# The order of a projection and mLSTM head loop, of an output projection and of a closing norm, rewritten; low halves and token shifts on GpSimd

## The chip, the cores and the metric

The program runs on one core of a Trainium2 chip. The metric is the device time of one execution in microseconds. An execution is one step of a small decoder layer over 576 tokens, 512 of a prompt and 8 sequences of 8 sample tokens.

## The reference, cut to what matters

```python
def mlstm_chunkwise(q, k, v, ig, lf, C0, n0, m0):      # per head and chunk of tokens
        m_t = jnp.maximum(log_inter, jnp.max(log_d, axis=-1))
        d = jnp.exp(log_d - m_t[..., None])
        s_inter = jnp.exp(log_inter - m_t)
        qk = jnp.einsum('bhtd,bhsd->bhts', qc, kc) * d
        num = s_inter[..., None] * jnp.einsum('bhtd,bhde->bhte', qc, C) + jnp.einsum('bhts,bhse->bhte', qk, vc)
        ...
        C_new = s_state[..., None, None] * C + jnp.einsum('bhs,bhsd,bhse->bhde', w_chunk, kc, vc)

def rwkv7_mixer(cols, shift0, S0, mu, ...):
    prev = jnp.concatenate([shift0[:, None, :], cols[:, :-1]], axis=1)
    xs = cols + (prev - cols) * mu                     # the token shift
    ...
    kk = kk / jnp.maximum(jnp.linalg.norm(kk, axis=-1, keepdims=True), 1e-12)

def hybrid_layer(x, ...):
    cols = (rmsnorm(x, norm_mix_g) @ w_in).astype(f32)
    ...
    x = x + mix @ w_out
    x = x + peer(rmsnorm(x, norm_ffn_g), peer_w_q, peer_sub_keys, peer_u, peer_v)
```

and at the end `y = rmsnorm(x, norm_final_g)`. Four mLSTM heads of width 128 and eight RWKV heads, worked in four pairs, share the input projection `w_in`. `peer` is a product-key mixture of single-row experts.

## The kernel before, in words

Activations stand transposed, channels on partitions and tokens along the free dimension. float32 products are taken as three products of a rounded high half and a low half: ScalarE writes the high half of a weight panel, another engine writes the low half as raw minus high.

**Stage A, the projection jobs and the heads.** The input projection is a list `JOBS`. The first 23 (`NF`) give q, k, v and o. The last 14 are of kind "r", one for each 128 RWKV columns; each is 48 matmuls of 128x288 on a narrow panel. There are two panel slots `narrow[0]` and `narrow[1]`: the load of panel j waits until job j-2 is done, `narrow_high` makes its high half on ScalarE and `narrow_low` its low half on VectorE (L1815). Every "r" job writes banks 0 and 1 and begins only when ScalarE has copied the bank of the job ahead of it (`copy_job`, L806 to L808). GpSimd then scales the copied columns by the rows' norm (L678, L679).

The list `BESIDE` says how many "r" jobs follow each part of the four heads. On TensorE a head is `decays` (six matmuls, L1226 to L1232), `keys` (transposes of the keys and the key-query products), `updates` (L1256, L1258), `numerators` (L1266 to L1271) and `head_back` (transposes, L1278). Between them VectorE does the state update (`cn`, `cnS`), the convolution of the next head (`conv`, L1893, L1895), the head norm's statistics and the product with `sg` (`silu`); ScalarE does the decay weights (exponentials, L876, L877), sigmoids (L815, L904), the norm's root (L913) and the normalised rows `hs_t` (L920). `decays(h + 1)` waits for `hs_ready` of head h, since it writes banks 2 and 3 that `hs_t` reads. In head 3 VectorE also makes the channel tensors of the first RWKV pair (`prep_first`: shifts, `decay_sums`, `kk_clamp`, a reciprocal at L1990, products up to L2011), ahead of the last two jobs' columns and behind them. The pair loop then begins with transposes (L1432, L1436) and the gram products (L1444). GpSimd makes the channel tensors of pairs 1 to 3 (`prep`).

**Stage B, the output projection.** Ten products of 8 matmuls each, first the left halves of the five token tiles (`FTILES`), then the right halves (L1635). VectorE adds each to the rows (L2311), then norms all tiles (L2316, L2319), TensorE transposes them (L1663), and the 16 query jobs follow (L1689, L1690).

**Stage C, the end.** The last expert sums run over eight column banks c = 0 to 7. VectorE copies each bank out (L2604), TensorE transposes all back (L1783), and per token tile VectorE adds two halves (L2614), ScalarE squares and takes a root (L1161, L1162), VectorE takes a reciprocal and scales (L2618, L2619), and a DMA writes the tile out. Engines run their own queues in the order in which the code is written; semaphores join them.

## Time and profile before

| | us |
|---|---|
| median of 3 runs (lowest, highest) | 2225.6 (2223.4, 2240.89) |
| the profiled execution, its own time | 2228.57 |
| its span, from the first to the last instruction | 2226.7 |
| mean granted clock of TensorE in it | 0.956 of full speed |

Times in the rows below are microseconds from the start of that span. A row of the timeline is: start, busy time, engine, line, operation, output and inputs, and in square brackets the idle time of the engine ahead of it with what ended it. "x48" is the number of instructions run together. The clock 1.0 stands for 2.4 GHz, 0.5 for 1.2 GHz; a number between them is a mean over a stretch.

### The profile page before, as it was taken

What the parts mean: (1) busy time and instruction counts of PE and PEld (TensorE: products, weight loads), DVE (VectorE), ACT (ScalarE), POOL (GpSimd) and SP (SyncE); (2) the same over time, 40 slices, a digit from 0 to 9 for tenths busy, and PEclk for the clock granted to TensorE, in tenths of its full rate; (3) what the DMA queues carried; (4) which work ended last, traced back from release to release, by engine and by line L of the source; (5) the groups of instructions that cost most, each with busy time, mean ns of one, the idle gap of its engine ahead of it and who ended that gap; (6) DMA issues with size and microseconds to landing.
All of it is one profiled execution on the core that took longest, in us unless ns stands there. A gap on an engine that the chain in (4) does not pass through costs nothing.

```text
span 2226.7 us, 35721 instructions
## 1 busy us (share of the span) xinstructions
PE 2072.9 (93%) x14513; PEld 1818.7 (82%) x14513; DVE 1549.0 (70%) x2689; ACT 752.3 (34%) x924; POOL 549.1 (25%) x473
## 2 busy tenths in 40 slices
PE   7999778778899998999999999999999999999995
PEld 7988657656646778888889889989899999999995
DVE  6435656556424888888898889897776666677664
ACT  5334334333112003334444544544322222222221
POOL 8111106541000000032242242122423233332320
PEclk9999868788999999999999999999999999999998
DMA  5121210002121213577797788679988888888872
GB/s 184 58 61 49 59 36 3 7 2 83 50 109 43 76 38 128 187 245 262 270 366 277 255 326 304 236 276 357 373 317 310 311 323 308 306 304 305 312 253 88
DMA packets 175771, 437.45 MB, mean 196 GB/s; under 512 B 12192, under 2 KB 92832, under 8 KB 165280
## 3 DMA queue, kind: packets, MB, share of 16 engines
q1 hardware_dynamic: 127552, 242.81, 31.5%
q0 software_dynamic: 36864, 134.23, 16.2%
q10 hardware_dynamic: 11232, 58.73, 6.5%
q8 instruction: 82, 1.34, 0.2%
q14 instruction: 41, 0.34, 0.0%
HBM read 368.57 MB, written 67.17 MB: 196 GB/s over the span
## 4 chain that ended last, share of the span: by engine, by line
PE 59%; DVE 11%; issue 1%; ACT 1%; DMA 0%; POOL 0%; ACTq 0%; DVEq 0%
PE bank L1770 28%; PE bank L1708 23%; PE bank L1717 3%; PE bank L1635 3%; DVE sc L2330 1%; DVE si L2329 1%; DVE si L2332 1%; DVE isel L2472 1%; DVE sv L2328 1%; DVE sv L2331 1%; DVE u_lo L2337 1%; DVE sca L2343 1%; DMA sca<-in_pu_rows,pick 0%; ACT u_hi L1068 0%; PE bank L1689 0%
## 5 line engine op out<-in xcount | busy, mean ns | idle before, releaser
L1708 PE MATMUL bank<-xhi,u_hi 128*128 128x448 f32 x1024 | 386.3, 377 | 8.8 <-DVE u_lo L2337 8.2
L1770 PE MATMUL bank<-w_hi,v_hi 128*128 128x448 f32 x1024 | 375.1, 366 | 5.5 <-DVE w_lo L2575 5.5
L1708 PE MATMUL bank<-xhi,u_lo 128*128 128x448 f32 x1024 | 375.9, 367 | 0.0
L1708 PE MATMUL bank<-xlo,u_hi 128*128 128x448 f32 x1024 | 375.2, 366 | 0.0
L1770 PE MATMUL bank<-w_lo,v_hi 128*128 128x448 f32 x1024 | 374.8, 366 | 0.0
L1770 PE MATMUL bank<-w_hi,v_lo 128*128 128x448 f32 x1024 | 374.8, 366 | 0.0
L725 POOL DMA_INDIRECT sca<-in_pu_rows,pick x128 | 169.8, 1326 | 733.2 <-DVE sdot L2343 447.2
L725 POOL DMA_INDIRECT rows_v<-in_pv,pick x128 | 196.4, 1535 | 430.6 <-DVE xs L2557 383.2
L2581 DVE TENSOR_TENSOR v_lo<-v_raw,v_hi 128x4096 fp32r<-128x4096 f32 x32 | 141.6, 4425 | 172.4 <-ACT v_hi L1129 172.4
L1129 ACT ACTIVATE v_hi<-v_raw 128x4096 fp32r<-128x4096 f32 x32 | 116.1, 3627 | 429.0 <-PE bank L1770 426.3
L1708 PEld LDWEIGHTS bank<-xhi,u_hi 128*128 128x128 f32 x1024 | 193.1, 189 | 24.1 <-issue 7.9
L1770 PEld LDWEIGHTS bank<-w_hi,v_hi 128*128 128x128 f32 x1024 | 193.0, 189 | 21.2 <-issue 5.9
L1708 PEld LDWEIGHTS bank<-xhi,u_lo 128*128 128x128 f32 x1024 | 193.8, 189 | 17.8
L1708 PEld LDWEIGHTS bank<-xlo,u_hi 128*128 128x128 f32 x1024 | 193.7, 189 | 15.3
L1770 PEld LDWEIGHTS bank<-w_lo,v_hi 128*128 128x128 f32 x1024 | 193.1, 189 | 15.3
L1770 PEld LDWEIGHTS bank<-w_hi,v_lo 128*128 128x128 f32 x1024 | 192.9, 188 | 15.3
L2337 DVE TENSOR_TENSOR u_lo<-u_raw,u_hi 128x2048 fp32r<-128x2048 f32 x64 | 146.5, 2290 | 61.9 <-ACT u_hi L1068 61.6
L1076 ACT ACTIVATE actb<-bank 128x448 f32<-128x448 f32 x128 | 69.8, 545 | 348.7 <-PE bank L1708 341.6
L2557 DVE SCALAR_TENSOR_TENSOR xs<-rows_v,sdot,xs 128x1024 f32<-128x1024 f32 x127 | 162.7, 1281 | 10.8 <-DMA rows_v<-in_pv,pick 3.7
L2343 DVE CUSTOM_DVE_ANT_0 sca<-sca,xs 128x1024 f32<-128x1024 f32 x128 | 151.7, 1220 | 19.0 <-DMA sca<-in_pu_rows,pick 18.6
L1068 ACT ACTIVATE u_hi<-u_raw 128x2048 fp32r<-128x2048 f32 x64 | 123.2, 1926 | 23.2 <-issue 9.1
L1097 ACT ACTIVATE gst<-bank 128x512 f32<-128x512 f32 x112 | 125.2, 1146 | 15.5 <-PE bank L1717 11.7
(619 smaller groups left out, 3486.4 us busy)
## 6 DMA issues: line engine op xcount, KB each, us to landing
u_raw<-in_pu SPq DMA_DIRECT2D x64, 1024.0 KB
v_raw<-in_pv SPq DMA_DIRECT2D x32, 2048.0 KB, 16.7
act_scratch<-actb ACTq DMA_DIRECT2D x64, 448.0 KB
gate_scratch<-gst ACTq DMA_DIRECT2D x14, 2048.0 KB, 9.1
wts<-act_scratch SPq DMA_DIRECT2D x32, 896.0 KB, 4.7
gring<-gate_scratch SPq DMA_DIRECT2D x32, 896.0 KB, 8.6
wring<-in_w_q SPq DMA_DIRECT2D x4, 2048.0 KB, 8.5
wp_raw<-in_w_in SPq DMA_DIRECT2D x7, 1024.0 KB, 5.5
```

What stands on the lines that cost most here:

```text
L725: pool.indirect_dma_start(dst, None, rows[:, :], bass.IndirectOffsetOnAxis(pick[:, s:s + 1], 0)).then_inc(s_row[s % RING], 16)
L1068: act.activation(u_hi[:, g % 2, :, :], u_raw[:, g % 2, :, :], ACT.Copy).then_inc(S("u_hi_ready"), 1)
L1076: act.activation(actb[:, q, e, :], bank[b][:, 0:DS], ACT.Gelu).then_inc(S("dot_banks_free"), 1)
L1097: act.activation(gst[:, c % 2, :, o:o + 4].rearrange("p a t -> p t a"), bank[5 + k % 2][:, :].rearrange("p (t a) -> p t a", t=4), ACT.Copy ...
L1129: act.activation(v_hi[g % 2][:, :], v_raw[g % 2][:, :], ACT.Copy).then_inc(S("v_hi_ready"), 1)
L1635: return mm(bank[jj % 6][0:n, :], mixT[:, kt, t0:t0 + n], w_o[:, half, kt, :], start=kt == 0, stop=kt == KD - 1)
L1708: ins = mm(bank[b][:, 0:DS], lhsT, rhs[:, 0:DS], **on)
L1770: ins = mm(bank[c][:, 0:DS], lhsT, rhs[q][:, e, :], **on)
L2337: TT(u_lo[:, g % 2, :, :], u_raw[:, g % 2, :, :], u_hi[:, g % 2, :, :].bitcast(f32), ALU.subtract).then_inc(S(f"u_lo_ready{g % 2}"), 1)
L2343: dve.tensor_tensor_reduce(rows_u[s % RING], rows_u[s % RING], xs[:, :], 1.0, 0.0, ALU.mult, ALU.add, sdot[:, s:s + 1]).then_inc(S("row_us ...
L2557: STT(out=accS[:, :], in0=rows_v[:, s % RING, :], scalar=sdot[:, s:s + 1], in1=accS[:, :], op0=ALU.mult, op1=ALU.add).then_inc(S("row_adde ...
L2581: TT(v_lo[q][:, :], v_raw[q][:, :], v_hi[q][:, :].bitcast(f32), ALU.subtract).then_inc(S("v_lo_ready"), 1)
```

## The change

**Stage A.** On TensorE, `decays(h + 1)` moves up behind `numerators(h)` and waits for `p_ready` and `cn_ready`; the numerators get banks 6 and 7. Head 3 has no jobs of its own: its two jobs run in head 2, with the first pair's small products `lora_decay` and `lora_rate` between them. In `keys` the products come first. The first pair's `bonus_sums` comes behind the transposes of the pair loop. On GpSimd come all 14 low halves, each ahead of the scaling of the job before, and the shifts of the first pair and of the two gate inputs; `prep_first` is gone, and what is left of it is written into head 3 on VectorE. On ScalarE the decay weights of head h + 1 and a high half come ahead of the root and `hs_t` of head h, and the copy of one job's bank comes behind `hs_t`.

**Stage B.** The output projection goes tile by tile, the adds, norms and transposes of a tile follow while the next is multiplied, and the first two query jobs are split into two token halves around the last two tiles' transposes.

**Stage C.** Token tile 4 is finished first, banks are turned back as they are copied, the left and right halves are squared apart, and ScalarE scales the left half.

```diff
@@ -665,40 +668,73 @@
 
             pool.wait_ge(s_low, LOW["rms"])
             rb_seq = rb[:, SEQ:NT].rearrange("p (b s) -> p b s", b=NB)
-            for ji, (kind, _, _, d) in enumerate(JOBS):
+            def narrow_low(j):
+
+                if j == 0:
+                    pool.wait_ge(s_low, LOW["w7"])
+                if j < 14:
+                    pool.wait_ge(s_high, HIGH[f"n{j}"])
+                    raw, hi, lo = narrow[j % 2]
+                    pool.tensor_tensor(lo[:, :, :], raw[:, :, :], hi[:, :, :].bitcast(f32), ALU.subtract).then_inc(s_low, 1)
+
+            TT, TSC = pool.tensor_tensor, pool.tensor_scalar
...
+            def shifted(dst, ct):
+                seq, own_seq = [a.rearrange("p (b s) -> p b s", b=NB) for a in (ext_r[:, ct, 1 + SEQ:], dst[:, SEQ:NT])]
+                cur, prev = ext_r[:, ct, 1:1 + SEQ], ext_r[:, ct, 0:SEQ]
+                TT(dst[:, 0:SEQ], prev, cur, ALU.subtract)
+                link(TT(own_seq, seq[:, :, 0:NS], seq[:, :, 1:], ALU.subtract))
+                link(TSC(dst[:, :], dst[:, :], pcol("mu", ct), None, ALU.mult))
...
+
+            for ji, (kind, i, _, d) in enumerate(JOBS):
                 if kind in "gv":
                     continue
+                if ji == FIRST[7]:
+                    narrow_low(0)
+                if kind == "r":
+                    narrow_low(i + 1)
                 pool.wait_ge(s_pe, ji + 1)
...
+                if kind == "r" and i in (1, 9, 10, 13):
+                    pool.wait_ge(S("scaled"), 12 + i + 1)
+                if kind == "r" and i == 1:
+                    pool.wait_ge(S("rows_ready"), 1)
+                    shifted(xwa, 12)
+                    shifted(xg, 13).then_inc(S("lora_in"), 1)
+                if kind == "r" and i == 9:
+                    pool.wait_ge(S("conv_ready"), 8)
+                    link(shifted(X["r"], 0))
+                if kind == "r" and i == 10:
+                    link(shifted(X["k"], 4))
+                    link(TSC(X["kk"][:, :], X["k"][:, :], pcol("k_k", 0), None, ALU.mult))
+                if kind == "r" and i == 11:
+                    TT(X["t"][:, :], X["kk"][:, :], X["kk"][:, :], ALU.mult).then_inc(S("kk_squares"), 1)
+            shifted(XP[0]["v"], 8)
+            pool.wait_ge(S("decay_ready"), 1)
+            TT(ARP[0][:, 1, :], X["r"][:, :], X["cum"][:, :], ALU.mult).then_inc(S("scaled"), 1)
+
...
             jobs = iter(range(NF, NJ))
-            for h in range(MLH):
+
+            def decay_weights(h):
                 act.wait_ge(S("decays_done"), h + 1)
...
+            decay_weights(0)
+            highs = iter(range(1, 14))
+            narrow_high(next(highs))
+            copy_job(next(jobs))
+            for h in range(MLH):
                 if h:
...
                     act.activation(mixT[:, 0:4, :], mixT[:, 0:4, :], ACT.Sigmoid)
-                if h == 2:
...
+                if h + 1 < MLH:
+                    decay_weights(h + 1)
+                    narrow_high(next(highs))
                 act.wait_ge(S("stats_step"), 2 * h + 1)
                 act.activation(sm[:, 3, :], sm[:, 2, :], ACT.Sqrt, bias=eps_t[:, 0:1]).then_inc(S("std_ready"), 1)
                 own(S("std_ready"))
...
@@ -917,18 +951,26 @@
                     act.wait_ge(S("head_back"), h)
                 for t, (t0, n) in enumerate(TILES):
                     o = 129 * (t % 3)
-                    last = act.activation(hs_t[0:n, t, :], bank[2 + t // 3][0:n, o:o + 128], ACT.Identity,
+                    last = act.activation(hs_t[0:n, t, :], bank[6 + t // 3][0:n, o:o + 128], ACT.Identity,
                                           scale=sm[0:n, 4, t:t + 1], bias=sm[0:n, 5, t:t + 1])
                 last.then_inc(S("hs_ready"), 1)
                 own(S("hs_ready"))
-                if BESIDE[h][3]:
-                    copy_r(next(jobs))
+                if h < 3:
+                    copy_job(next(jobs))
+                    narrow_high(next(highs))
+                if h == 2:
+                    lora(1, "sw", "w0", 0)
+                if h < 3:
+                    copy_job(next(jobs))
+                if h == 2:
+                    lora(2, "av", "a0", 0)
+                    copy_job(next(jobs))
...
+                act.wait_ge(S("y_ready"), t + 2)
+                act.activation(x1_late[t][0:n, halves[0]], y_half[t][0:n, :], ACT.Copy, scale=st[0:n, t, 3:4]
                                ).then_inc(S("yrms_ready"), 1)
                 own(S("yrms_ready"))
+            for t, (t0, n) in enumerate(FTILES[0:4]):
+                act.wait_ge(S("x2_ready"), t + 6)
+                link(act.activation(sq_late[0:n, halves[1]], x1_late[t][0:n, halves[1]], ACT.Square, accum_out=st[0:n, t, 0:1]))
+                act.activation(st[0:n, t, 3:4], st[0:n, t, 0:1], ACT.Sqrt, bias=st[0:n, t, 2:3], scale=1.0 / D
+                               ).then_inc(S("yrms_ready"), 1)
+                own(S("yrms_ready"))
+                if t:
+                    half_out(t - 1)
+            half_out(3)
 
...
             def keys(h):
                 pe.wait_ge(S("qk_ready"), h + 1)
+                pe.wait_ge(S("qs_ready"), h + 1)
+                for t, (t0, n) in enumerate(TILES):
+                    dst = bank[2][:, 128 * t:128 * t + 128] if t < PT else bank[3][0:n, 0:n]
+                    ins = mm(dst, kh[:, t0:t0 + n], qh[:, t0:t0 + n], start=True, stop=True)
+                ins.then_inc(S("qk_done"), 1)
...
+                    dst = bank[6 + t // 3][0:n, 129 * (t % 3):129 * (t % 3) + 129]
...
             jobs = iter(range(NF, NJ))
             decays(0)
+            job(next(jobs))
             for h in range(3):
-                for part, n_jobs in zip((None, keys, updates, numerators), BESIDE[h]):
-                    if part:
-                        part(h)
-                    for _ in range(n_jobs):
-                        job(next(jobs))
+                keys(h)
+                job(next(jobs))
+                updates(h)
+                job(next(jobs))
+                numerators(h)
                 decays(h + 1)
+                job(next(jobs))
+                if h == 2:
+                    lora_decay(0)
+                job(next(jobs))
+                if h == 2:
+                    lora_rate(0)
+                    job(next(jobs))
                 head_back(h)
-
-            early = prep(0)
-            next(early)
             keys(3)
-            next(early)
-            next(early)
+            kk_sums(0)
+            pe.wait_ge(S("kk_stage"), 1)
             updates(3)
-            pe.wait_ge(S("lora_out"), 2)
-            job(next(jobs))
-            next(early)
             numerators(3)
-            pe.wait_ge(S("kk_stage"), 1)
...
+                if p == 0:
+                    pe.wait_ge(S("mix_ready"), 4)
+                    bonus_sums(0)
...
+                t, half = divmod(jj, 2)
...
             pe.wait_ge(S("mix_ready"), 8)
+            def turn_back(t):
+
+                n = FTILES[t][1]
+                pe.wait_ge(S("xf_ready"), t + 1)
+                if t == 1:
+                    pe.wait_ge(S("x1_ready"), 6)
+                if t >= 2:
+                    pe.wait_ge(S("xfT_ready"), t - 1)
+                for kt in range(KD):
+                    ins = pe.transpose(bank[6 - 2 * (t % 2) + kt // 4][:, n * (kt % 4):n * (kt % 4) + n],
+                                       xf_rows(t)[0:n, 128 * kt:128 * kt + 128], ident[0:n, 0:n])
+                ins.then_inc(S("xfT_done"), 1)
+
...
                 for kt in range(KD - 1 if jj < 6 else 0, KD):
                     ins = out_product(jj, kt)
                 ins.then_inc(S("outproj_done"), 1)
-            for t, (t0, n) in enumerate(FTILES):
-                pe.wait_ge(S("xf_ready"), t + 1)
-                if t >= 2:
...
+            def q_half(j, half):
...
+            for j in range(2):
+                q_half(j, 0)
+                turn_back(3 + j)
             pe.wait_ge(S("xfT_ready"), 5)
-            pe.wait_ge(S("x1_ready"), 10)
...
+                q_half(j, 1).then_inc(S("qproj_done"), 1)
             def scores(j):
...
@@ -1769,6 +1883,15 @@
                                       skip_group_check=True)
                             ins = mm(bank[c][:, 0:DS], lhsT, rhs[q][:, e, :], **on)
                     ins.then_inc(S("sum_done"), 1)
+                    if last and c == 4:
+                        pe.wait_ge(S("sum_banks_free"), 4)
+                        for t in range(4):
+                            turn_half(t, range(0, 4), 0).then_inc(S("back_done"), 1)
+                    if last and c == 6:
+                        pe.wait_ge(S("sum_banks_free"), 6)
+                        pe.wait_ge(S("x2_ready"), 5)
+                        for t in range(4):
+                            turn_half(t, range(4, 6), 1)
...
+                turn_half(t, (6,), 1)
             pe.wait_ge(S("sum_banks_free"), KD)
-            for t, (t0, n) in enumerate(FTILES[0:4]):
...
+                turn_half(t, (7,), 1).then_inc(S("back_done"), 1)
 
 
...
+            add_rows(0)
+            add_rows(1)
+            add_rows(2)
+            dve.wait_ge(s_sub, 32)
+            norm_rows(0)
+            norm_rows(1)
+            add_rows(3)
+            norm_rows(2)
+            norm_rows(3)
+            add_rows(4)
+            norm_rows(4)
...
+            for c in range(1, 5):
+                bank_out(c)
+            for t in range(4):
+                add_half(t, 0)
+            for t in range(4):
+                n = FTILES[t][1]
+                TT(y_half[t][0:n, :], x1_late[t][0:n, 0:512], gain[0:n, 0:512], ALU.mult)
+                if t in (0, 2):
+                    bank_out(5 + t // 2)
+            bank_out(7)
+            add_half(0, 1)
+            for t in range(1, 4):
+                add_half(t, 1)
+                scale_rows(t - 1, slice(512, D), ROOT[t])
+            scale_rows(3, slice(512, D), ROOT[4])
 
 
```

TensorE's queue from the last products of numerators(0) on, before (L1178 is a job, L1226 to L1232 are decays(1), L1278 is head_back(0)):

```order
L1178 MATMUL bank<-xhi_b,wn_lo 128x288 x2
L1226 MATMUL bank<-row_E,selr 128x512 [waits cn_ready,hs_ready]
L1227 MATMUL bank<-row_E,selr 128x64
L1228 MATMUL bank<-row_E,selr 128x512
L1229 MATMUL bank<-negm,ident 128x512
L1231 MATMUL bank<-row_E,selr 64x64
L1232 MATMUL bank<-negs,ident 64x64
L1278 MATMUL bank<-ident,hs_t 128x128 [waits hs_ready]
```

The same place after; the job (L1255) now follows decays(1), which no longer waits for `hs_ready`:

```order
L1343 MATMUL bank<-vaug,dpm 64x129
L1348 MATMUL bank<-cn,qsX 64x129 x8
L1303 MATMUL bank<-row_E,selr 128x512 [waits cn_ready,p_ready]
L1304 MATMUL bank<-row_E,selr 128x64
L1305 MATMUL bank<-row_E,selr 128x512
L1306 MATMUL bank<-negm,ident 128x512
L1308 MATMUL bank<-row_E,selr 64x64
L1309 MATMUL bank<-negs,ident 64x64
L1255 MATMUL bank<-xlo,wn_hi 128x288 [waits proj_copied,low_halves_ready]
```

The decays moved ahead of one job, and head_back(0) stands behind that and another one.

ScalarE's queue behind the convolution of head 1, before (`mixT` is the output gate's sigmoid, `sm` the norm's root, `dpm` the decay weights, `wn_hi` a high half, `ext_r` a job's copy):

```order
L904 ACTIVATE mixT<-mixT 128x2304 [waits scaled,conv_sig]
L913 ACT_TABLE_LOAD
L913 ACTIVATE sm<-sm,eps_t 128x5 [waits stats_step]
L920 ACTIVATE hs_t<-bank,sm 128x128 [waits stats_step,std_ready]
L920 ACTIVATE hs_t<-bank,sm 128x128 x3
L920 ACTIVATE hs_t<-bank,sm 64x128
L763 ACTIVATE wn_hi<-wn_raw 128x1024 [waits w_narrow_loaded0,hs_ready]
L806 ACTIVATE ext_r<-bank 128x288 [waits proj_done]
L807 ACTIVATE ext_r<-bank 128x224
L808 ACTIVATE ext_r<-bank 128x8x8
```

and after:

```order
L935 ACTIVATE mixT<-mixT 128x2304 [waits scaled,conv_sig]
L908 ACT_TABLE_LOAD [waits p_ready]
L908 ACTIVATE dpm<-bank,mcol 128x128 [waits decays_done]
L908 ACTIVATE dpm<-bank,mcol 128x128 x3
L909 ACTIVATE dpm<-bank,mcol 64x64
L799 ACTIVATE wn_hi<-wn_raw 128x1024 [waits w_narrow_loaded0,d_ready]
L947 ACT_TABLE_LOAD
L947 ACTIVATE sm<-sm,eps_t 128x5 [waits stats_step]
L954 ACTIVATE hs_t<-bank,sm 128x128 [waits stats_step,std_ready]
L954 ACTIVATE hs_t<-bank,sm 128x128 x3
L954 ACTIVATE hs_t<-bank,sm 64x128
L842 ACTIVATE ext_r<-bank 128x288 [waits proj_done,hs_ready]
```

The exponentials and a high half stand ahead of the root, and a job's copy stands behind `hs_t` and waits for `hs_ready`.

GpSimd's queue around the second "r" job; before, only L678 and L679 stood here:

```order
L678 TENSOR_TENSOR wn_lo<-wn_raw,wn_hi 128x1024 [waits high_halves_ready]
L705 TENSOR_TENSOR ext_r<-ext_r,rb 128x512 [waits proj_copied]
L706 TENSOR_TENSOR ext_r<-ext_r,rb 128x8x8
L685 TENSOR_TENSOR xwa<-ext_r 128x512 [waits rows_ready,scaled]
L686 TENSOR_TENSOR xwa<-ext_r 128x64
L687 TENSOR_SCALAR xwa<-xwa,par 128x576 [waits gpsimd_step]
L688 TENSOR_TENSOR xwa<-xwa,ext_r 128x512 [waits gpsimd_step]
L689 TENSOR_TENSOR xwa<-xwa,ext_r 128x64
```

A low half, the job's scaling, and then two shifts of five operations each, the first of which is shown.

## Rows read from the trace of the kernel before

**Rows 1.** The page, busy time of each engine over the whole span

```profile
PE 2072.9 (93%) x14513; PEld 1818.7 (82%) x14513; DVE 1549.0 (70%) x2689; ACT 752.3 (34%) x924; POOL 549.1 (25%) x473
```

**Rows 2.** Windows: length, busy PE, PEld, DVE, ACT, POOL, clock, DMA share, GB/s

```profile
137.00:146.00 9.00, 8.89 (x55) 8.89 (x56) 3.73 (x9) 2.65 (x8) 0.00 (x0) 0.77 0.04 12
156.54:204.78 48.24, 43.82 (x282) 38.23 (x281) 25.42 (x64) 19.95 (x39) 6.41 (x8) 0.89 0.20 58
204.78:252.93 48.15, 43.83 (x281) 38.02 (x280) 29.83 (x71) 17.82 (x38) 6.39 (x8) 0.89 0.20 56
252.93:340.51 87.58, 64.95 (x363) 53.44 (x364) 54.80 (x135) 30.08 (x59) 9.41 (x11) 0.75 0.14 43
322.00:338.00 16.00, 3.60 (x15) 2.26 (x14) 12.82 (x21) 0.78 (x3) 2.04 (x2) 0.61 0.25 86
678.00:690.00 12.00, 7.77 (x46) 6.52 (x47) 7.72 (x12) 7.81 (x14) 0.00 (x0) 0.86 0.55 199
2198.00:2227.00 29.00, 3.95 (x34) 3.45 (x32) 14.28 (x21) 8.50 (x16) 0.00 (x0) 0.64 0.22 81
```

**Rows 3.** Timeline of PE in the projection and head loop

```profile
137.11 0.85 PE L1178 MATMUL bank<-xlo,wn_hi 128*128 128x288 f32 x2 [1.68 <-DVE wn_lo L1815]
...
153.58 1.05 PE L1256 MATMUL bank<-wv,ktok 128*128 128x129 f32 x8
...
156.54 0.53 PE L1178 MATMUL bank<-xlo,wn_hi 128*128 128x288 f32 x2
...
163.02 0.61 PE L1266 MATMUL bank<-vaug,dpm 128*128 128x129 f32 x4
...
177.98 1.47 PE L1226 MATMUL bank<-row_E,selr 4*128 4x512 f32 x2 [4.42 <-ACT hs_t L920]
...
279.45 2.07 PE L1226 MATMUL bank<-row_E,selr 4*128 4x512 f32 x2 [7.46 <-ACT hs_t L920]
```

**Rows 4.** Timeline of ACT behind head 0 and in front of head 1

```profile
171.58 2.13 ACT L904 ACTIVATE mixT<-mixT 128x2304 f32<-128x2304 f32 x1
...
176.09 1.83 ACT L920 ACTIVATE hs_t<-bank,sm 128x128 f32<-128x128 f32 x5 [0.78 <-DVE sm L2120]
...
184.47 1.28 ACT L876 ACT_TABLE_LOAD   x1 [4.79 <-issue]
185.76 1.14 ACT L876 ACTIVATE dpm<-bank,mcol 128x128 f32<-128x128 f32 x4
```

**Rows 5.** Timeline of DVE, head 0 and then head 3

```profile
160.33 1.23 DVE L1815 TENSOR_TENSOR wn_lo<-wn_raw,wn_hi 128x1024 fp32r<-128x1024 f32 x1
...
164.41 1.14 DVE L1893 TENSOR_SCALAR pre<-ext_q,par 128x64 f32<-128x64 f32 x1
...
169.50 0.31 DVE L1893 TENSOR_SCALAR pre<-ext_q,par 128x64 f32<-128x64 f32 x1
...
170.80 0.16 DVE L2102 COPY den<-bank 128x3 f32<-128x3 f32 x1
...
319.71 3.75 DVE L1990 RECIPROCAL rw_t<-rw_t 128x576 f32<-128x576 f32 x1
...
334.45 0.82 DVE L2011 SCALAR_TENSOR_TENSOR rw_t<-rw_r,par,rw_k 128x576 f32<-128x576 f32 x1
```

**Rows 6.** Timeline of POOL, two-input operations at three places

```profile
69.63 2.80 POOL L678 TENSOR_TENSOR ext_q<-ext_q,rb 128x512 f32<-128x512 f32 x1 [3.26 <-ACT ext_q L808]
...
164.07 1.43 POOL L678 TENSOR_TENSOR ext_r<-ext_r,rb 128x512 f32<-128x512 f32 x1 [8.08 <-ACT ext_r L808]
...
338.73 1.04 POOL L687 TENSOR_TENSOR cn<-ext_r 128x512 f32<-128x512 f32 x1 [13.45 <-DVE mixT L1942]
```

**Rows 7.** Timeline of DVE and PE at the end of the program

```profile
2198.28 0.62 DVE L2604 COPY mixT<-bank 128x448 f32<-128x448 f32 x1 [1.81 <-PE bank L1770]
...
2198.96 3.71 PE L1783 MATMUL bank<-ident,mixT 128*128 128x128 f32 x32 [0.72 <-DVE mixT L2604]
...
2222.42 1.28 DVE L2619 SCALAR_TENSOR_TENSOR v_raw<-v_raw,st,gain 128x1024 f32<-128x1024 f32 x1
```

More of the change, by code:

```diff
@@ L1312, in prep @@
                     pe.wait_ge(S("gate_out"), p - 1)
-                main_and_rest(blk[:, :], X["t"], "bonus_done")
+                channel_product(p, blk[:, :], X["t"], "bonus_done", rest_of(1))
+            def prep(p):
+                lora_decay(p)
+                yield
+                yield
+                lora_rate(p)
+                yield
+                kk_sums(p)
+                for _ in range(14):
+                    yield
+                bonus_sums(p)
                 yield
@@ L2186, in post @@
                 yield
-            for _ in early:
-                pass
+            bonus(0)
             c_md = 0
@@ new lines, in scale_rows, with add_half @@
+            def scale_rows(t, cs, root):
+                n = FTILES[t][1]
+                dve.wait_ge(S("yrms_ready"), root)
+                link(dve.reciprocal(st[0:n, t, 3:4], st[0:n, t, 3:4]))
+                STT(out=x1_late[t][0:n, cs], in0=x1_late[t][0:n, cs], scalar=st[0:n, t, 3:4], in1=gain[0:n, cs], op0=ALU.mult,
+                    op1=ALU.mult).then_inc(S("y_ready"), 1)
+                own(S("y_ready"))
+            def add_half(t, half):
+                n, cs = FTILES[t][1], slice(512 * half, 512 * half + 512)
+                dve.wait_ge(S("back_done"), 4 * half + t + 1)
+                TT(x1_late[t][0:n, cs], bank[t][0:n, :], x1_late[t][0:n, cs], ALU.add).then_inc(S("x2_ready"), 1)
+                own(S("x2_ready"))
```

352 lines of the change are left out of this document (143 added, 209 removed).

## The prediction

> **What bounds the kernel now.** I read the page first: TensorE is busy for 93% of the span [rows 1]. The rest is the budget of any reordering: idle time, and time at the lower clock. So I went to the windows and looked only at the stages that the diff touches [rows 2]. The projection and head loop costs 48.24, 48.15 and 87.58 us for three parts, cut where the `updates` of heads 0, 1 and 2 end and at the first gram product. TensorE is idle for 4.4, 4.3 and 22.6 us of them, and the clock is 0.89, 0.89 and 0.75. Last I read on the timeline what ended each idle time [rows 3]. It is the same in each head: `decays(h+1)` waits for `hs_t`, 4.42 us at 177.98 and 7.46 at 279.45. At 137.11 the first job waits 1.68 for its low half. From 322 to 338 TensorE works 3.60 of 16 us, under VectorE's products for the first pair. Stage B holds 4.2 idle us between 678 and 690, stage C has 3.95 of work in 29 [rows 2].
>
> **The durations I use.** A job is 6.48 us at the full clock (156.54 to 163.02), `updates` 2.96 (153.58 to 156.54), and one pass of 128 columns 0.131 (1.05 for 8) [rows 3]; so `keys` with 15 passes is about 2.0 and `head_back` with 5 about 0.65, both estimates. A restart after a gap also costs clock: the nine microseconds from 137 have a mean of 0.77, so 4.1 us ran at 1.2 GHz and about 2.0 us of work were lost [rows 2]. I take 1.75 for a job that follows an idle time.
>
> **Stage A, the start: −3.5.** The low half of the first panel is now made on GpSimd before TensorE needs it, so the wait of 1.68 goes, and with it most of the 2.0 of slow clock. Nothing else is due there.
>
> **Stage A, head 0: +2.1.** `decays` no longer waits for `hs_t`. But the fourth job of a head needs a bank that ScalarE copies behind `hs_t`, and so the wait returns one job and one `decays` later. What counts is the chain from the end of `updates` to that copy. VectorE: from 156.54 to 170.80 it makes the state and the convolution, 14.26 us; the low half of 1.23 leaves it and so does 0.83 of the row at 164.41 (1.14, where the same operation takes 0.31 at 169.50), so 12.2 [rows 3, 5]. ScalarE: the sigmoid of 0.78 up to 171.58, `mixT` 2.13, the decay weights that now come ahead (table load 1.28, exponentials 1.14, with the small one 2.6), a high half of 1.1 (estimate from `mixT`, 1024 of 2304 columns), table load, root and wait 2.38 up to 176.09, `hs_t` 1.83, the copy 0.8 (estimate, as the sigmoid of 576 columns): 11.6 [rows 4]. To this comes what GpSimd takes from VectorE. The rows at 164 show an exclusion: GpSimd's scaling took 1.43 there, the same kind 1.04 alone at 338.73 and 2.80 at 69.63, and VectorE's row at 164.41 lost 0.83 [rows 5, 6]. In head 0 GpSimd now has, beside the convolution, the four two-input operations of the second shift (estimate 2.7, twice 1.04 and twice a small one), a low half (2.2, an estimate from 1.04 for 512 columns) and a scaling (1.4): 6.3. I take all of it as lost. The chain is 12.2 + 6.3 + 11.6 = 30.1, against some 21 of TensorE's own work, so it stands for nine. Behind it come a job, `head_back`, `keys`, a job and `updates`, 18.6 by the durations above, and 1.75 of clock: 50.4 against 48.24 [rows 2]. Bounds: 44.1 with no exclusion (−4.2), and 53.9 if the slow clock lasts as it does now: 0.11 of 48.24 is 5.3 [rows 2], 3.5 more than 1.75 (+5.6).
>
> The Trainium skill, page "SBUF — State Buffer", section "Who interferes with whom", says that VectorE and GpSimd share one pair of ports and that it is "an exclusive lock": two-input VectorE instructions meet GpSimd's reads there, and those in a two-port mode block it for the whole instruction. The rows agree, in both directions (1.14 for 0.31, 2.80 for 1.04) [rows 5, 6]. The rule speaks against the change, which sends two-input work to GpSimd beside VectorE's own. By the rule head 0 comes to +2.1, as in my sum; without it, to −4.2.
>
> **Stage A, head 1: −2.0.** The same chain with 3.0 of exclusion (a low half, 0.8 of a scaling) and 10.8 on ScalarE, where the two gate inputs take the place of `mixT`: 12.2 + 3.0 + 10.8 + 18.6 + 1.75 = 46.3, against 48.15 [rows 2]. Bounds −5 and +1.7.
>
> **Stage A, heads 2 and 3 to the first gram product: −13.8.** Now four jobs (25.9) run behind head 2's `updates`, and with `numerators`, `decays`, the small products, `head_back`, `keys` and about 1 of waiting (together 16.6, estimates by passes) TensorE reaches `updates(3)` after 42.5. From there the way is serial: `updates` 3.0, the state 3.7, the reciprocal of 3.75 and three products of 0.8 [rows 5], 6.7 with the waits; statistics, root, three more products and `hs_t`, 8.1; then `head_back`, the transposes, `bonus_sums` and 2.5 for a slow clock, 9.8. That is 73.8 against 87.58 [rows 2]. The gain comes from two places: the two jobs that stood in head 3 at half clock now run at full clock without a gap, and the shifts of the first pair and `AR[:,1]` no longer stand in VectorE's row up to 334.45 [rows 5]. Bounds: 68 (VectorE's products hidden under `updates`) and 80 (the low clock lasts).
>
> Of GpSimd's later duty: `prep(1)` starts 2.8 later against the first gram, since the first pair's `bonus` now gates it together with the transposes. I put +1.0 there, between 0 and 2. **Stage A in all: −3.5 + 2.1 − 2.0 − 13.8 + 1.0 = −16.2**, with −23 and −8 as ends that do not all fall together.
>
> **Stage B: −2.7.** Of 12.00 us TensorE works 7.77 [rows 2]. The waits for all adds, then for all norms, go; the two query halves run beside the last tiles' transposes. What cannot go is the last tile's add, root, norm, transposes and copy; beside them there are two half query jobs of about 2.6 us together. I leave 1.5 idle. Bounds −1 (the halves wait as long for the third tile's columns) and −4.5.
>
> **Stage C: −13.2.** Before, the last copy ends at 2198.90 and five rounds of add, square, root and scale are serial through two engines, until 2223.70; the span ends 3.0 later, with the DMA [rows 7]. After, 24 of 32 transposes stand ahead of the last bank's sums, 2.8 of 3.71 [rows 7]: this is a cost, since TensorE is the bound there. The copy ends at 2201.7, the last four transposes 0.8 later, the first half add (0.65, half of 1.28) at 2203.2. Then ScalarE is the bound: it is busy for 8.50 in this window for five tiles with a table load [rows 2], so 1.44 a tile; the half that it no longer squares is replaced by the half that it scales, and I add 0.35 for waits, 1.8. Four tiles end at 2210.5, the DMA at 2213.5, against 2226.7. Bounds: 1.5 a tile (−14.4), 2.3 a tile (−11.2).
>
> **The sum** is −16.2 − 2.7 − 13.2 = −32.1, so 2196.5 for an execution like the profiled one of 2228.57. The median lies 3.0 below that one, so **2193.5**.
>
> **Rivals.** *The wait in the heads only moves.* The new wait behind `hs_t` is as long as the old one, the clock falls and comes back as slowly as now, so that each of three heads costs 3.5 more: −21.6, 2204. For it: nine idle us in head 0 are twice 4.42, and the restart at 177.98 was slow [rows 2, 3]. Against it: what follows the gap is now a dense job instead of small products. 0.2. *GpSimd and VectorE do not exclude each other in these places*, by chance of timing: 6.3 + 3.0 less, 2184. For it: the row of 1.43 is only 0.4 longer than 1.04 [rows 6]. 0.13. *GpSimd's low halves become the bound (slower).* A job waits for its low half. The price: a low half of 2.2 has some 2 us of slack where two jobs follow each other; if each were stretched as the row of 2.80 is against 1.04 [rows 6], by 2.7, it would take 5.9, and 14 of them would cost 14 × 1.7 = 24 us. The change turns to a loss from 6.5 us each on; at 7.5 it costs 46, and the time is 2240. Against it: VectorE is busy for 25.42 of 48.24 us only [rows 2], so that no low half finds it at work all the time. 0.04, a third of it within 1%. The forecast keeps 0.63.
>
> **Range and chances.** A measurement here tells 1% from nothing, so faster means under 2203.3. The forecast and the second rival lie under it with nearly all their mass, the first rival with half. Faster 0.84, within 1% 0.13, slower by over 1% 0.03. For the range I leave out one tenth at each side: from the second rival, 2182, to a little over the first, 2209.
>
> **What would show it.** In the profile after: no wait at the first job; `decays(1)` directly behind `numerators(0)` and a wait of the fourth job of head 0 of about nine us, ended by ScalarE's copy; about five in head 1; clock 1.0 over the three jobs around `lora_decay`; VectorE's convolution and GpSimd's shifts each longer than alone; the first gram product some 17 us earlier; `updates(3)` some 42 us behind `updates(2)`; the last ScalarE scaling about 12 us behind the last sums. I am wrong if a job waits for GpSimd's low half for more than a microsecond in several places, if the clock stays at 1.2 GHz through whole jobs behind the new gap, or if the 24 transposes ahead of the last sums wait for VectorE's copies.

## The result and the profile after

The changed kernel took 2197.28 us (median of 4, 2196.28 to 2205.4), the kernel before 2227.78 in the same sets; the ratio is 0.9861 with a 95% interval of 0.9813 to 0.991. The span of the profiled execution fell from 2226.7 to 2196.0, by 30.7. In four of the fourteen profiles an untouched stretch in the middle lasts some 12 us longer (last section), so below I compare stages, and medians only beside them.

The page of the kernel after, busy time of the engines (against [rows 1]):

```profile
PE 2070.0 (94%) x14513; PEld 1823.0 (83%) x14513; DVE 1528.4 (70%) x2655; ACT 758.2 (35%) x940; POOL 606.2 (28%) x515
```

Windows of the kernel after, cut at the same events as [rows 2]: the start of job 0, from `updates(0)` to `updates(1)`, to `updates(2)`, to the first gram product, the pair loop to the output projection, stage B to the first scores, the untouched middle, and the end from the fourth copied bank. The columns are those of [rows 2].

```profile
134.00:143.00 9.00, 9.00 (x46) 8.62 (x46) 3.76 (x11) 3.66 (x7) 2.37 (x1) 0.64 0.04 12
155.09:204.61 49.52, 43.92 (x281) 39.61 (x281) 24.97 (x60) 20.06 (x39) 24.62 (x22) 0.86 0.20 55
204.61:249.50 44.89, 41.99 (x281) 38.52 (x280) 30.18 (x71) 19.19 (x40) 15.73 (x12) 0.92 0.22 61
249.50:320.27 70.77, 57.43 (x366) 49.75 (x366) 36.71 (x103) 30.04 (x59) 30.86 (x30) 0.88 0.17 53
320.27:629.03 308.76, 251.38 (x4229) 195.11 (x4229) 165.19 (x328) 92.05 (x217) 98.49 (x78) 0.84 0.08 27
629.03:686.40 57.37, 53.38 (x181) 28.70 (x182) 14.30 (x21) 12.93 (x27) 0.24 (x1) 1.00 0.38 142
686.40:2170.61 1484.21, 1466.60 (x8062) 1321.45 (x8061) 1174.62 (x1951) 509.44 (x420) 365.77 (x256) 0.99 0.73 266
2170.61:2196.00 25.39, 13.50 (x80) 12.03 (x78) 14.66 (x25) 11.03 (x28) 0.00 (x0) 0.85 0.20 72
```

And the windows of the kernel before for the stretches that [rows 2] do not show in this cut: pair loop, stage B, middle, end.

```profile
340.51:643.95 303.44, 244.17 (x4239) 187.34 (x4235) 164.28 (x326) 93.13 (x220) 95.65 (x76) 0.87 0.08 28
643.95:704.28 60.33, 55.61 (x180) 30.78 (x181) 14.30 (x21) 16.12 (x28) 0.24 (x1) 0.97 0.36 135
704.28:2188.55 1484.27, 1465.81 (x8062) 1321.52 (x8061) 1172.21 (x1947) 503.25 (x415) 366.22 (x256) 0.99 0.73 265
2188.55:2226.70 38.15, 13.40 (x80) 12.09 (x78) 16.78 (x25) 8.50 (x16) 0.00 (x0) 0.73 0.17 62
```

| stage | before | after | difference | forecast |
|---|---|---|---|---|
| start, to the end of `updates(0)` | 156.54 | 155.09 | −1.4 | −3.5 |
| head 0 | 48.24 | 49.52 | +1.3 | +2.1 |
| head 1 | 48.15 | 44.89 | −3.3 | −2.0 |
| heads 2 and 3, to the first gram | 87.58 | 70.77 | −16.8 | −13.8 |
| pair loop | 303.44 | 308.76 | +5.3 | +1.0 |
| stage B | 60.33 | 57.37 | −3.0 | −2.7 |
| middle | 1484.27 | 1484.21 | −0.1 | 0 |
| end | 38.15 | 25.39 | −12.8 | −13.2 |
| sum | 2226.7 | 2196.0 | −30.7 | −32.1 |

The timeline of TensorE after, where [rows 3] show it before:

```profile
134.95 0.85 PE L1255 MATMUL bank<-xlo,wn_hi 128*128 128x288 f32 x2
...
170.23 0.85 PE L1255 MATMUL bank<-xlo,wn_hi 128*128 128x288 f32 x2
...
184.43 0.82 PE L1255 MATMUL bank<-xlo,wn_hi 128*128 128x288 f32 x2 [5.60 <-ACT ext_r L844]
...
229.75 0.82 PE L1255 MATMUL bank<-xlo,wn_hi 128*128 128x288 f32 x2 [2.90 <-ACT ext_r L844]
...
299.86 1.20 PE L1343 MATMUL bank<-vaug,dpm 128*128 128x129 f32 x4 [3.88 <-DVE cnS L2132]
...
313.81 1.41 PE L1355 MATMUL bank<-ident,hs_t 128*128 128x128 f32 x5 [7.79 <-ACT hs_t L954]
...
667.59 2.66 PE L1764 MATMUL bank<-mixT,wring 128*128 128x288 f32 x10 [2.76 <-ACT mixT L1094]
...
678.53 8.03 PE L1764 MATMUL bank<-mixT,wring 128*128 128x288 f32 x32 [1.23 <-ACT mixT L1094]
```

The wait of 1.68 at the first job is gone, those of `decays` for `hs_t` too. What came in their place is at 184.43 and 229.75: the job behind the one that follows `decays` waits for ScalarE's copy. Here and in the experiments I call these two the fourth and the fifth job of a head, counting the job ahead of `keys` as the first; the prediction counted from the one behind `keys`, so its "fourth job of head 0" is the fifth here. Head 3 keeps two waits, 3.88 for the state and 7.79 for `hs_t`. The job at 170.23 follows no idle time and still lasts until 178.83, 8.60 instead of 6.6.

VectorE after, from the end of `updates(0)`, and below it GpSimd beside it:

```profile
155.27 0.29 DVE L2125 COPY cn<-bank 128x129 f32<-128x129 f32 x1 [9.10 <-PE bank L1335]
...
159.53 3.34 DVE L2013 SCALAR_TENSOR_TENSOR pre<-ext_q,par,pre 128x512 f32<-128x512 f32 x3
162.91 0.45 DVE L2011 TENSOR_SCALAR pre<-ext_q,par 128x64 f32<-128x64 f32 x1
163.40 3.78 DVE L2013 SCALAR_TENSOR_TENSOR pre<-ext_q,par,pre 128x64 f32<-128x64 f32 x3
167.21 1.39 DVE L2011 TENSOR_SCALAR pre<-ext_q,par 128x512 f32<-128x512 f32 x1
...
172.30 0.16 DVE L2149 COPY den<-bank 128x3 f32<-128x3 f32 x1
```

```profile
159.15 1.24 POOL L685 TENSOR_TENSOR xg<-ext_r 128x512 f32<-128x512 f32 x1
...
161.19 2.13 POOL L687 TENSOR_SCALAR xg<-xg,par 128x576 f32<-128x576 f32 x1
163.40 1.09 POOL L688 TENSOR_TENSOR xg<-xg,ext_r 128x512 f32<-128x512 f32 x1
...
164.72 2.37 POOL L678 TENSOR_TENSOR wn_lo<-wn_raw,wn_hi 128x1024 fp32r<-128x1024 f32 x1
```

From the end of the updates at 155.09 to 172.30 VectorE takes 17.2 us, for the work of 12.2 in the prediction: three operations on 64 columns take 3.78 (0.92 in the kernel before) and lie over GpSimd's two-input operations at 163.40 and 164.72; one of 0.55 takes 1.39 and lies over the scaling behind them. GpSimd's own rows at 159.15 and 161.19 are longer than alone too (1.24 for 1.04, 2.13 for 1.72).

The end after, VectorE's last copy and ScalarE's last scaling:

```profile
2183.05 0.62 DVE L2678 COPY mixT<-bank 128x448 f32<-128x448 f32 x1 [2.10 <-PE bank L1884]
...
2191.85 0.72 ACT L1230 ACTIVATE v_raw<-v_raw,st 64x512 f32<-64x512 f32 x1 [0.37 <-DVE v_raw L2685]
```

### The profile page after: what moved, and what is told of

It reads as the page before. It is cut to its first block, busy times and chain, and to the rows that moved or that the text cites. A ratio compares the mean times of both kernels' runs of the same rounds, so it can differ in the third digit from the quotient of the medians.

```text
span 2196.0 us, 35764 instructions
## 1 busy us (share of the span) xinstructions
PE 2070.0 (94%) x14513; PEld 1823.0 (83%) x14513; DVE 1528.4 (70%) x2655; ACT 758.2 (35%) x940; POOL 606.2 (28%) x515
## 4 chain that ended last, share of the span: by engine, by line
PE 59%; DVE 11%; ACT 1%; issue 1%; DMA 0%; POOL 0%; ACTq 0%; DVEq 0%
PE bank L1884 28%; PE bank L1814 22%; PE bank L1823 3%; PE bank L1721 3%; DVE sc L2403 1%; DVE si L2402 1%; DVE si L2405 1%; DVE u_lo L2410 1%; DVE isel L2545 1%; DVE sv L2401 1%; DVE sv L2404 1%; PE bank L1764 1%; DVE sca L2416 1%; DMA sca<-in_pu_rows,pick 0%; ACT u_hi L1123 0%
## 5 line engine op out<-in xcount | busy, mean ns | idle before, releaser
L1814 PEld LDWEIGHTS bank<-xhi,u_lo 128*128 128x128 f32 x1024 | 193.7, 189 | 17.9
## 6 DMA issues: line engine op xcount, KB each, us to landing
v_raw<-in_pv SPq DMA_DIRECT2D x32, 2048.0 KB, 16.9
```

What stands on the lines that cost most here:

```text
L1814: ins = mm(bank[b][:, 0:DS], lhsT, rhs[:, 0:DS], **on)
```

## The experiments

Each is the changed kernel with one edit, unless it says otherwise; L-numbers are those of its own file.

**1 (e1). Stage A as before, B and C as changed.** All edits of the input loop, the heads and the first pair were taken back.

> The head loop and everything up to the first pair as before the change; stages B and C as changed. Theory (the parts add up, and the pair loop gives back some 5 us of stage A's 20 by its clock): B is worth 3.0 and C 12.8, so 2227.8 - 15.8 = 2212. Rival (the give-back in the pair loop came with B or C, or is chance of that one profile, and A is worth 20): then the median lies near 2217. In the profile the stretch from the first gram product to the output projection should be 303 us, as before, by the theory.

Measured: 2219.15 (median of 10, 2210.09 to 2225.5), span 2211.0 with a middle of 1483.9. The median alone is nearer to the rival's 2217 than to 2212, but the ten times scatter over 15 us, so I go by the profile, and there the sum by stages is the theory's: the span is 15.0 above that of the changed kernel and 15.7 under the one before. Stage B took 57.37 and the end 25.4, as in the changed kernel. The first gram product came 20.9 later than there, and the stretch from it to the first scores took 360.6, where the changed kernel took 366.1. So in these two profiles A is worth 15 of the 30.7. The 5 us in the pair loop are not B's or C's, but that they come from A's edits is not shown: experiments 6, 8 and 9, with A in, took 360.3 to 360.6 there as well.

**2 (e2). Stage C as before.**

> Only stage C (the end) as before. Theory: 12.8 of the gain is this stage and nothing else depends on it, so 2197.3 + 12.8 = 2210. Rival (the 24 transposes ahead of the last bank's sums cost more than they bring, and the end would be as good with only the halves): under 2206.

Measured: 2210.97 (median of 9, 2205.77 to 2223.7). The end took 38.37 from the fourth copied bank instead of 25.39: 13.0, as expected. The rival is out. Up to the last expert sums this program has the same instructions as the changed kernel, and two stretches came out differently all the same: head 0, and the one from the first gram product to the first scores (366.13 in the changed kernel).

```profile
154.38:204.93 50.55, 41.89 (x282) 38.42 (x281) 24.98 (x60) 20.07 (x39) 24.64 (x22) 0.90 0.19 54
321.18:684.82 363.64, 299.51 (x4409) 217.94 (x4409) 178.50 (x349) 105.01 (x244) 98.31 (x79) 0.88 0.13 45
```

**3 (e3). Low halves back on VectorE.**

```diff
-                if ji == FIRST[7]:
-                    narrow_low(0)
-                if kind == "r":
-                    narrow_low(i + 1)
...
+                if h < 3:
+                    narrow_low(4 * h + 3)        # on VectorE, behind the state of a head
```

> Only the 14 low halves go back to VectorE, 1.23 each, all else as changed. Theory (port exclusion makes the move worth nothing: VectorE loses as much time to GpSimd's 2.37 us subtraction as its own took): within 2 us of 2197, with the first job waiting 1.7 again. Rival (relieving VectorE is where stage A's gain comes from): 5 us or more slower, 2202 to 2207, with jobs waiting for low halves.

```profile
136.01 0.85 PE L1242 MATMUL bank<-xlo,wn_hi 128*128 128x288 f32 x2 [0.82 <-DVE wn_lo L1925]
```

Measured: 2205.83 (median of 4, 2190.37 to 2208.1), with the longer middle (1496.7) in its profile. The median lies in the rival's range, but 12.5 us of the profiled time are that middle, which no low half touches. The first gram product came at 320.86 against 320.27: head 0 1.3 shorter, head 1 the same, the last part 2.1 longer. By these stages the theory's size holds: moving 14 subtractions to GpSimd moved the first gram product by 0.6 us. Its reason, the exclusion, is not tried by this run. The first job waits 0.82, less than I said.

**4 (e4). A copy ahead of the root.**

```diff
                     decay_weights(h + 1)
                     narrow_high(next(highs))
+                    copy_job(next(jobs))
...
                 if h < 3:
-                    copy_job(next(jobs))
                     narrow_high(next(highs))
```

> Only ScalarE's order: the copy of the bank of a head's fourth job stands ahead of the root and of the normalised rows instead of behind them. Theory (the new waits of 5.60 and 2.90 us are the place of the copy in ScalarE's queue): both fall under 1 us, and the head periods by 4 and 2 us, so 2190 to 2192. Rival (the wait only moves on, to head_back or the keys, since the normalised rows come 1 us later and VectorE's next head with them): within 1.5 us of 2197.

```profile
180.85 0.85 PE L1255 MATMUL bank<-xlo,wn_hi 128*128 128x288 f32 x2 [5.61 <-POOL wn_lo L678]
...
177.33 1.06 ACT L799 ACTIVATE wn_hi<-wn_raw 128x1024 fp32r<-128x1024 f32 x1
```

Measured: 2196.4 (median of 4, 2185.27 to 2198.38), with a middle of 1496.4 in the profile, so the rest of the span is 12.1 shorter. Head 0 took 47.3 (−2.2), head 1 40.5 (−4.4); 3.8 of the 12.1 lie behind the first gram product. In head 1 the theory is right, the wait fell to 1.37 and the clock stayed at 1.0. In head 0 the wait is as long as before, but another ends it: the low half on GpSimd, 2.34 us behind a high half that ScalarE makes at 177.33 behind the gate sigmoid and the decay weights. Neither theory had that.

**5 (e5). The changed kernel once more.**

> The changed kernel once more. It asks whether the granted clock between the first gram product and the output projection (262.8 us in the first profile, 256.5 before the change) is a property of the kernel. Theory (it is chance: the same instructions meet another phase of the clock): this profile gives another value, between 256 and 262, while the head periods 49.5 and 44.9 come back within 1.5. Rival (the new order of the first pair costs the pair loop 5 us): 262 to 263 again.

```profile
155.94:205.59 49.65, 44.02 (x282) 39.92 (x281) 24.97 (x60) 20.08 (x39) 24.57 (x22) 0.86 0.19 54
205.59:250.56 44.97, 42.03 (x281) 38.56 (x281) 30.29 (x71) 19.21 (x40) 15.84 (x12) 0.92 0.22 61
321.25:687.40 366.15, 304.83 (x4410) 224.00 (x4409) 179.39 (x349) 105.11 (x244) 98.80 (x79) 0.86 0.13 45
```

The 262.8 and 256.5 in it end at the first output matmul that is issued inside the pair loop, ahead of the cut of the table.

Measured: 2197.7 (two runs). Head periods within 0.15, and the stretch from the first gram product to the first scores 366.15 against 366.13. The value came back, against what the theory (chance) said. But that the clock there belongs to the kernel is not shown either: experiment 2, with the same instructions up to there, took 363.64, and over the whole span the two executions whose profiles are compared here had a mean granted clock of 0.961 and 0.960, the other four of the same program 0.965 to 0.967. The time up to `updates(0)` did not come back, 155.94 against 155.09.

**6 and 7 (e6, e12). The gate inputs' shifts one and two jobs later** (`i == 1` becomes `i == 2`, then `i == 3`).

> Only the two shifts of the gate inputs on GpSimd come one job later, behind the third RWKV job instead of the second, so that they no longer stand beside the convolution of head 1. Theory (port exclusion cost VectorE 5.0 us in head 0, half of it by these shifts): VectorE's way from the end of the updates to the statistics falls from 17.2 to about 15, and head 0's period from 49.5 to about 47.5. Rival (what VectorE loses there is hidden behind ScalarE): the period stays at 49 or more.

> Only the two shifts of the gate inputs again, now behind the fourth RWKV job's scaling, some 184 us into the span. In e6 they still stood beside the convolution, which ran until 171.8. Theory (VectorE's 5.0 us of loss in head 0 are port exclusion, and 3.5 of them by the shifts): VectorE's way from the end of updates(0) to the statistics falls from 17.2 to 13.5 to 14.5, the fifth job begins at 181 to 182 instead of 184.4, head 0 takes 46 to 47.5. Rival (the loss has another cause, or the low half and the scaling then take their place): the way stays above 16.

Measured: 2194.02 and 2193.0 (two runs each). At `i == 2` the shifts ran from 163.9 to 173.8, still beside the convolution: VectorE's way stayed at 16.9, head 0 at 49.10, and my expectation was wrong in its timing. At `i == 3`, VectorE, TensorE and GpSimd:

```profile
168.43 0.16 DVE L2149 COPY den<-bank 128x3 f32<-128x3 f32 x1
```

```profile
180.56 0.82 PE L1255 MATMUL bank<-xlo,wn_hi 128*128 128x288 f32 x2 [5.25 <-ACT ext_r L844]
...
193.38 0.55 PE L1255 MATMUL bank<-xlo,wn_hi 128*128 128x288 f32 x2 [2.21 <-POOL wn_lo L678]
```

```profile
189.66 1.09 POOL L688 TENSOR_TENSOR xg<-xg,ext_r 128x512 f32<-128x512 f32 x1
190.71 0.31 POOL L689 TENSOR_TENSOR xg<-xg,ext_r 128x64 f32<-128x64 f32 x1
190.98 2.34 POOL L678 TENSOR_TENSOR wn_lo<-wn_raw,wn_hi 128x1024 fp32r<-128x1024 f32 x1
```

The way is now 154.69 to 168.43, 13.7, as the theory says, and the fifth job begins 3.9 earlier. But head 0 is no shorter, 49.71: the shifts stand at 182 to 191 ahead of the low half in GpSimd's queue, the next job (193.38) waits 2.21 for it, and it lasts 8.15 instead of 6.59, since the clock fell to 1.2 GHz from 193.8 to 197.2. So two things are shown: standing beside the convolution the shifts cost VectorE 3.5 us (17.2 against 13.7), and GpSimd's queue has too little slack for ten more operations between these two low halves.

**8 (e7). Numerators, job, decays, job.** TensorE's order and, with it, ScalarE's (high half, copy, decay weights).

```diff
                 numerators(h)
-                decays(h + 1)
                 job(next(jobs))
+                decays(h + 1)
```

> TensorE's order is numerators, job, decays, job; ScalarE copies the first of these jobs ahead of the decay weights. Theory (the gap of head 0 comes from what stands ahead of the copy and of the next high half on ScalarE, not from TensorE's order): with the decay weights (2.6 us) out of that chain the gap of 5.6 shrinks to 1 to 2, and head 0 takes 42 to 45 us, head 1 40 to 42. Rival (the decays come later, so do the normalised rows, and the wait moves to head_back or keys): head 0 at 47 or more, as with the copy alone moved (47.3).

Measured: 2188.32 (two runs), head 0 44.6, head 1 40.7. The wait ahead of the fifth job is 1.17. The theory holds; in head 0 a job of 9.2 us remains, behind a wait. The last part grew from 70.8 to 75.1.

**9 (e8). The same, with the high half ahead of the convolution's sigmoid and the shifts at `i == 2`.**

> The order of the run before, the shifts one job later, and the high half of the fifth panel of a head ahead of the convolution's sigmoid instead of behind the gate sigmoid. Theory (with the copy moved, the job waited for GpSimd's low half, which waits for that high half): no wait over 1.5 us is left ahead of a job; head 0 at 41 to 43, head 1 at 40 to 41, the whole 12 to 16 us under the changed kernel when the untouched middle is equal. Rival (the chain through VectorE to the next head's keys bounds the head at about 45): 6 to 8 us under it.

Measured: 2190.56 (median of 4, 2182.91 to 2203.14), span 2181.6 with a middle of 1484.5, so 14.4 under the changed kernel, as the theory says; two of the four times lie at 2197.8 and 2203.1, and no profile shows why. Head 0 40.84, head 1 40.68, both at a clock of 1.00. The last part stayed at 75.0: its first small product now waits for the decay weights of head 3.

```profile
260.31 2.04 PE L1359 MATMUL bank<-xwa,w 64*128 64x512 f32 x2 [2.83 <-ACT dpm L909]
```

**10 (e9). One joined job back into head 3**, in the changed kernel.

```diff
             updates(3)
+            job(next(jobs))
             numerators(3)
```

> The changed kernel with its last projection job back in head 3, between updates(3) and numerators(3), where TensorE waits 3.9 us for VectorE. Theory (the joined jobs are not what made the last part 16.8 us shorter; VectorE's shortened serial work is): the job fills that wait, keys(3) comes 6.6 earlier and the numerators 6.6 instead of 3.9 behind the updates, so the last part falls from 70.7 to 67 to 68. Rival (joining the jobs is the gain, since a job in head 3 runs at the low clock, or its columns then come too late for GpSimd's shift of v): 72 to 76.

```profile
311.20 1.41 PE L1355 MATMUL bank<-ident,hs_t 128*128 128x128 f32 x5 [11.07 <-ACT hs_t L955]
```

Measured: 2193.87 (two runs). The last part took 69.33, 1.4 less than with the jobs joined. The sign is the theory's, the size is not: the wait of 3.88 is filled, and 11.07 instead of 7.79 are then waited for `hs_t`, since the numerators end 2.7 later. Joining that job was not the gain; it cost a little.

**11 (e10). Heads 0 and 1 as in 9, head 2 as changed** (decays ahead of the job).

> As e8 in heads 0 and 1, but head 2 keeps the decays ahead of the job, so that the decay weights of head 3 no longer hold up the first small product of the pair (2.8 us in e8). Theory: heads 0 and 1 at 40.8 and 40.7 again, the last part at 69.5 to 71 instead of 75.0. Rival (the late decays in head 2 were not its cause): 75 again.

```profile
154.94:195.54 40.60, 39.24 (x282) 35.70 (x281) 27.30 (x60) 19.94 (x39) 24.65 (x22) 1.00 0.24 67
195.54:237.70 42.16, 42.16 (x282) 37.87 (x281) 32.68 (x71) 19.21 (x40) 15.98 (x12) 0.92 0.23 65
237.70:309.16 71.46, 56.92 (x367) 49.32 (x366) 36.73 (x103) 30.03 (x59) 31.58 (x29) 0.88 0.17 53
309.16:671.99 362.83, 299.00 (x4410) 217.53 (x4409) 178.25 (x349) 104.98 (x244) 98.13 (x79) 0.89 0.13 45
```

Measured: **2182.4** (median of 4, 2179.09 to 2183.21), ratio to the kernel before 0.9765 (0.9728 to 0.9802): the lowest median of this study, some 15 under the changed kernel. Head 0 40.60 at clock 1.00, head 1 42.16, the last part 71.46. So the late decays in head 2 were the cause of the 75.0.

**12 (e11). 10 and 11 together.**

> The two before together. Theory (the gains lie in separate stages and add): heads 0 and 1 at 40.8 and 40.7, the last part at 66 to 68, so that everything up to the first gram product is 16 us shorter than in the changed kernel, and the median near 2181 where the middle runs as fast. Rival (with less idle time ahead of it the pair loop pays it back by its clock): the pair loop takes over 262 us and the median lies at 2187 or above.

Measured: 2187.28 (median of 6, 2180.26 to 2198.9); three of the six lie at 2180 to 2182. Its profile has the longer middle. Head 0 41.56, head 1 40.67, the last part 70.63, 12.8 less up to the first gram product than the changed kernel instead of 16. The stretch from there to the first scores took 366.9 (362.8 in 11), so the 1.7 gained over version 11 before the first gram product went in the pair loop, and 2.4 more. The rival's numbers came, in one profile; its reason is not shown, since experiment 9, with its first gram product at 311.6, took 360.3 for the same stretch.

## Why the prediction was right, and where it was not

The sum was off by 1.4 (−30.7 against −32.1), and part of that is luck: the last part and head 1 gained 3.0 and 1.3 more than forecast, the start gained 2.1 less and the pair loop lost 4.3 more, and these errors nearly cancel.

*Stage A, start.* −1.4 against −3.5. The wait went as said, the slow clock did not: job 0 lasted 9.15 us. The step that failed is "with it most of the 2.0 of slow clock": I had put the low clock down to the wait. The windows at 1.2 GHz, before and after:

```profile
134.25:141.08 6.83, 5.15 (x21) 4.54 (x21) 6.33 (x13) 3.66 (x7) 0.00 (x0) 0.50 0.05 16
133.72:140.55 6.83, 6.83 (x28) 6.17 (x28) 4.04 (x11) 3.66 (x7) 1.66 (x1) 0.50 0.05 16
```

Both last 6.83 us, and both begin ahead of the wait, while `decays(0)` still runs (in both kernels TensorE had been idle for 0.91 ahead of `decays(0)`). So the wait of 1.68 lay inside the slow stretch, and without it more of job 0 ran there. That the wait itself is not fixed shows in experiment 1: with stage A as before it was 0.12, job 0 took 9.21, and the start 156.3. Elsewhere too the clock fell without idle time: the fourth job of head 0 took 8.60, in a stretch at 1.2 GHz from 167.9 to 174.7, with TensorE busy without a break from 130.8 on. The same instructions do not always do it: that job took 6.61 in experiments 2 and 4. What decides is open.

*Head 0.* +1.3 against +2.1. The chain to the copy took 29.3 against 30.1 (155.1 to 184.4): the exclusion 5.0 against 6.3. But TensorE's own work was slower (the job of 8.60 and, ahead of it, 1.1 more in `decays`), so the idle time was 5.60, not nine, at nearly the same total. That GpSimd's operations lengthen VectorE's is shown by experiment 7 (13.7 instead of 17.2). The Trainium skill, page "SBUF — State Buffer", section "Who interferes with whom", says that a two-input VectorE instruction contends with a GpSimd instruction that reads SBUF; the trace agrees (3.78 for 0.92). That the new wait stood behind ScalarE's order is shown by 4, 8 and 9.

*Head 1.* −3.3 against −2.0 (the prediction's own terms add up to −1.8); the wait was 2.90, not five.

*The last part.* −16.8 against −13.8, the largest error among the heads. `updates(3)` came 43.4 behind `updates(2)`, as said (42.5). The serial rest took 27.4 instead of 31.3: I had given 2.5 to a slow clock and too much to the products, of which only the reciprocal and four others lay ahead of the statistics. My reason named two sources. The first, two jobs "at half clock", was misread: before, they took 8.17 and 6.62, and experiment 10 refutes it for one of the two joined jobs (back in head 3 it took 6.61). Nor did the clock stay at 1.0 over the three jobs around `lora_decay`, as the prediction's list of signs had it: the first took 7.86. The second source, VectorE's shorter serial way, is argued from the timelines (the wait for the product `rw_t` below is gone) and was not tried alone.

```profile
335.32 2.08 PE L1285 MATMUL bank<-rw_t,blk 128*128 128x512 f32 x2 [12.39 <-DVE rw_t L2011]
```

*The pair loop.* I forecast +1.0 from a later start of GpSimd's `prep(1)`; it was +5.3. TensorE was idle for 57.4 instead of 59.3 there and busy for 251.4 instead of 244.2 with the same products, at a mean clock of 0.84 instead of 0.87. So it is the clock and not a wait: the step that failed is that I gave this stage a wait alone and put its clock at nothing. With the same code in that loop, the stretch to the first scores took between 360.3 and 366.9 in twelve profiles, and 363.6 and 366.1 with the same instructions ahead of it too (experiments 2 and 5). What decides is open.

*Stage B.* −3.0 against −2.7, a right number for a reason that was mostly wrong. Idle time fell by only 0.7 (4.7 to 4.0): the waits of 2.76 and 1.23 for ScalarE's copies replaced the old ones, as my bound of −1 had it. The rest came from the clock, 0.97 to 1.00. All thirteen profiles with the new stage B took 57.4, so the 3.0 are the stage's own.

*Stage C.* −12.8 against −13.2. The last copy ended at 2183.67, in the old frame (17.9 later) 2201.6 for the 2201.7 forecast; ScalarE's four rounds took 7.7, 1.92 each against 1.8; the span ended 3.4 behind them, not 3.0. The 24 transposes did not wait for VectorE. The sign "about 12 us behind the last sums" was off: the last scaling ended 9.5 behind them, and the prediction's own times give 9.

*The rivals.* The wait did move: TensorE's idle time in heads 0 and 1 went from 4.42 and 4.32 to 5.60 and 2.90, now ahead of a job instead of small products. The job behind it was slow even so, 8.35 and 7.92 for 6.6. GpSimd as the bound did not show in the changed kernel; it did as soon as ScalarE's wait was taken away (4) or its queue was loaded (7).

## What to carry to other kernels

When a wait is moved, ask what stands ahead of its new releaser in that engine's queue: here a copy and a high half behind work that nobody yet waited for cost as much as the wait that was removed, and placing them earlier, with the small products split, gave 12 us more in two heads (experiment 11). Two-input work sent to GpSimd beside two-input work on VectorE brought less than a microsecond here; count it twice, or put it where VectorE waits. Do not put a low clock down to the wait next to it before looking at when it fell. With a job between `numerators` and `decays` both heads ran at 1.00 in experiment 9, but not in 8, 11 and 12, where one of them had 0.92 to 0.96, so that this order does it is not shown.

## What the runs showed that I had not expected

The middle, from the first scores to the last sums, has two lengths in the same code: 1483.9 to 1485.0 us in ten profiles of this study, 1496.4 to 1496.9 in four others (experiments 2, 3, 4 and 12). The difference lies in the last expert sums and is even: in stretches of 20 us there are 98 or 99 matmuls in place of 100 or 101, at a granted clock of 1.00 in both and without idle time. Whether the executions that show no profile differ by the same thing can't be seen; those of the kernel before, with 1484.3 in its profile, lie between 2223 and 2243. Here is that window in experiment 4:

```profile
674.40:2170.77 1496.37, 1477.78 (x8062) 1321.16 (x8061) 1174.67 (x1951) 509.41 (x420) 367.60 (x256) 0.99 0.72 263
```

VectorE, ScalarE and GpSimd are busy for the same time in both. Nothing in the traces explains it, and it stays open. It is larger than several of the effects studied here, so single times and small medians can't tell these versions apart. The stages of a profile can, down to the 2.5 us by which the same instructions differed between experiment 2 and the changed kernel.
